# A two-block transformer step on one core: the ring of streamed weights, six slots of 1 MB or four

## What is computed

```python
# block 1: modulation from c; then, on h = norm(x) * (1 + scale) + shift
proj   = h @ w_in                       # 1024 x 7712, in column groups
y_att  = attention(q, k, v)             # 8 heads, keys of latent and context
y_gla  = gated_linear_attention(...)    # 4 heads, both directions
y_hy   = hyena_mix(u)                   # 2 long convolutions, as DFT products
x      = x + gate * (sum_b sigmoid(g_b) * (y_b @ w_br_b)) @ w_out
x      = x + gate * grouped_moe(h2)     # 16 experts, 3 matrices of 1024 x 512 each, top 2
# block 2
y_lru  = (gelu(h @ w_g) * rg_lru(conv(h @ w_x))) @ w_lru_out
y_dil, y_mem = dilated attention, attention over a memory of 256 tokens
x      = x + (gated sum of the three) @ w_out
x      = x + square(relu(hm @ w_mlp_in)) @ w_mlp_out     # 1024 x 4096 x 1024
return rms_norm(x)
```

## Time and profile before

| what | value |
|---|---|
| median of 3 runs | 2804.03 us (2803.7 to 2805.57) |
| the profiled execution: its own time | 2803.01 us |
| its span, first to last instruction | 2801.2 us |
| busy, share of the span | PE 88%, PEld 56%, DVE 40%, ACT 28%, POOL 12% |
| mean granted clock of PE, share of full | 0.92 |
| moved by DMA | 303.32 MB, mean 108 GB/s |
| DMA engines busy in the expert stage (slices 20 to 23 of 40) | 90% or more |

### The profile page before, as it was taken

The page is one execution under the profiler, slowest core; times in us unless marked ns, Lnnn a source line. Parts: engine busy times, 40 slices in busy tenths (PEclk is TensorE's granted clock), DMA queues, the critical chain, the costliest instruction groups (busy, mean ns, idle before and its releaser), DMA issues. The chain is left out here.

```text
span 2801.2 us, 22860 instructions
## 1 busy us (share of the span) xinstructions
PE 2464.0 (88%) x9040; PEld 1580.9 (56%) x9040; DVE 1110.4 (40%) x1481; ACT 772.2 (28%) x1070; POOL 327.4 (12%) x132
## 2 busy tenths in 40 slices
PE   5998989998989999885999738999869998499997
PEld 2446634543433666564887624445636666388885
DVE  2134376621423322225988641521562223522223
ACT  3131113212111211124877521520521112222121
POOL 0000000000000222211000000000012222344340
PEclk9996899999989899987999959999969999799999
DMA  5203113311111222205999921132102222232200
GB/s 202 96 31 153 39 60 123 118 53 35 38 34 53 83 90 90 90 31 213 378 394 394 369 69 51 60 109 60 46 21 70 94 87 75 66 114 87 93 31 30
DMA packets 177753, 303.32 MB, mean 108 GB/s; under 512 B 10205, under 2 KB 67592, under 8 KB 177652
## 3 DMA queue, kind: packets, MB, share of 16 engines
q1 hardware_dynamic: 171988, 283.07, 28.9%
q0 software_dynamic: 3360, 10.48, 1.1%
q10 hardware_dynamic: 2304, 8.39, 0.7%
HBM read 278.78 MB, written 23.13 MB: 108 GB/s over the span
## 5 line engine op out<-in xcount | busy, mean ns | idle before, releaser
L190 PE MATMUL ps<-region 128*128 128x512 f32 x1024 | 411.1, 401 | 79.2 <-DVE region L2771 35.5
L180 PE MATMUL ps<-region,weights 128*128 128x512 f32 (+3 forms) x1056 | 436.8, 573 | 34.3 <-PEq L376 17.9
L192 PE MATMUL ps<-region 128*128 128x512 f32 x1024 | 404.0, 395 | 0.0
L191 PE MATMUL ps<-region 128*128 128x512 f32 x1024 | 403.3, 394 | 0.0
L180 PEld LDWEIGHTS ps<-region,weights 128*128 128x128 f32 (+1 forms) x1056 | 198.4, 190 | 263.4 <-issue 255.9
L172 PE MATMUL ps<-region,weights 128*128 128x512 f32 x720 | 321.5, 602 | 3.0 <-DVE region L1421 3.0
L190 PEld LDWEIGHTS ps<-region 128*128 128x128 f32 x1024 | 195.7, 191 | 125.0 <-POOL region L1504 39.0
L1993 DVE TENSOR_TENSOR region<-weights,region 128x2048 fp32r<-128x2048 f32 x96 | 217.4, 2288 | 53.1 <-ACT region L1932 52.7
L172 PEld LDWEIGHTS ps<-region,weights 128*128 128x128 f32 x720 | 136.2, 192 | 169.2 <-issue 164.5
L192 PEld LDWEIGHTS ps<-region 128*128 128x128 f32 x1024 | 195.2, 191 | 42.1
L191 PEld LDWEIGHTS ps<-region 128*128 128x128 f32 x1024 | 196.1, 191 | 38.8
(11 more groups left out here) (348 smaller groups left out, 2645.5 us busy)
## 6 DMA issues: line engine op xcount, KB each, us to landing
weights<-w_in SPq DMA_DIRECT2D x54, 1024.0 KB, 5.2
weights<-moe_w_gate SPq DMA_DIRECT2D x32, 1024.0 KB, 13.0
weights<-moe_w_up SPq DMA_DIRECT2D x32, 1024.0 KB, 13.5
weights<-moe_w_down SPq DMA_DIRECT2D x32, 1024.0 KB, 12.9
weights<-w_mod SPq DMA_DIRECT2D x24, 1024.0 KB, 5.4
weights<-w_mlp_in SPq DMA_DIRECT2D x16, 1024.0 KB, 5.2
weights<-w_mlp_out SPq DMA_DIRECT2D x16, 1024.0 KB, 5.0
h_slots<-region SPq DMA_DIRECT2D x16, 512.0 KB
```

The costliest lines, as they stand in the source:

```text
L180: ins = pe.matmul(out, w[:, k % 4, col:col + m], x[:, k, tokens], start=(k == 0), stop=(k == KD - 1))
L190: pe.matmul(out, w_hi, x_hi, start=(n == 0), stop=False)
L191: pe.matmul(out, w_hi, x_lo, start=False, stop=False)
L192: last = pe.matmul(out, w_lo, x_hi, start=False, stop=(n == len(triples) - 1))
```

## The change

The ring gets four slots in place of six, and the wait of the MLP's loop on a slot's arrival counts the uses of a slot in one round of the loop from RING: 12 chunks in four slots are three uses (48) where they were two (32).

```diff
@@ -20,7 +20,7 @@
 CT = NCTX // P
 EPS = 1e-6
 HALF = 512
-RING = 6
+RING = 4
 NMARKS = 16
 NSIG = 24
 
@@ -2731,7 +2731,7 @@
         def _(act):
             def high(c, i):
                 n = n0 + c
-                act.wait_ge(r.arrived[n % RING], i * 32 + r.arrival(n))
+                act.wait_ge(r.arrived[n % RING], i * (16 * BC // RING) + r.arrival(n))
                 if c >= CH:
                     act.wait_ge(spent, i * BC + c - CH + 1)
                 act.activation(flat(part(c, 0)), raw(c)[:, :], ACT.Copy).then_inc(w_hi_done, 1)
```

## The result

| | before | after |
|---|---|---|
| median, range (4 runs each) | 2803.86 us (2801.22 to 2805.57) | 2834.97 us (2831.97 to 2838.28) |
| the profiled execution: time, span | 2803.01, 2801.2 us | 2833.9, 2832.1 us |
| busy PE, mean granted clock | 88%, 0.922 | 87%, 0.922 |

The ratio is 1.0112, with a 95% interval of 1.0095 to 1.0130: slower by 31 us. The forecast was 2831, with a range of 2817 to 2848. The page of after, as the earlier trace rows: the same instructions, and in the four slices of the expert stage 361 to 383 GB/s where 369 to 394 stood.

What follows compares the result with a forecast made beforehand. PE was taken to bound nearly everywhere, the weight stream perhaps in the expert stage. Opening 0.6, Hyena 14.1, recurrent 9.0 and expert 3.6 sum to 27.3 us on 2803.0, forecast as a 2831 us median; range 2817 to 2848.

Steps and rivals of the forecast that it cites:

- The rule k + 2: Whole ring: chunk k is issued when chunk k + 2 was before; hidden in projection, merge and MLP stages.
- The wait for Si: Hyena stages: Si is issued only after C, Sm and Ed are released; PE starts each inverse transform 4.8 us late.
- Its clock: Hyena stages: PE runs at its lower clock behind each gap before the inverse transform, 2.9 us each, bounds 0 and 5.
- Small loads: Start of the recurrent stage: small loads on SP land behind 2 MB of weights instead of 1 MB, +1.0 us.
- Second group: Recurrent stage: all four chunks of the second group are issued only when the first group is released, +3.0 us.
- qm: Recurrent stage: the two chunks qm are issued at the second release and land later than PE wants them, +3.0 us.
- The clock's +2.0 behind qm: Recurrent stage: two idle gaps close together before qm's matmuls lower PE's clock, +2.0 us, bounds 0 and 3.4.
- The 5.3 us of the two chunks: Expert stage: it starts with four chunks instead of six, so 92 instead of 90 are streamed in it, +5.3 us.
- Kept full, with 0.7 us to spare: Expert stage: a slot's round of 9.9 us against 10.6 us until its next chunk is due keeps the stream full.
- the stream runs thin: Expert stage rival: DVE and ACT hold slots too long, often one chunk under way; +15 us, 2846 us, chance 0.13.
- The gather: End of the expert stage: fewer chunks queued behind the last weight, so the gather waits less, -2.7 us.
- The opening stage: Opening stage: x comes after the fourth chunk, leaving PE more to do when the last lands, +0.6 us.

Runs made afterwards that it cites:

- w4_dft: Kernel before (six slots), but the chunks of the two Hyena stages issued only four ahead; 2814.91 us, ratio 1.0043.
- w4_lru: Kernel before (six slots), but the chunks of the recurrent stage, with the two of qm, issued only four ahead; 2808.64 us, ratio 1.0019.
- w5_moe: Kernel before (six slots), but the chunks of the expert stage issued only five ahead; 2807.31 us, ratio 1.0008.
- w4_moe: Kernel before (six slots), but the chunks of the expert stage issued only four ahead; 2818.84 us, ratio 1.0054.
- w3_moe: Kernel before (six slots), but the chunks of the expert stage issued only three ahead; 2854.37 us in its one run, beside 2802.38.
- rows_late4: Changed kernel, but in the expert stage DVE splits the next chunk before the rows of the next expert; 2830.71 us, ratio 1.0112.
- no_si: Changed kernel, but the Hyena inverse transform reads Ci in place of Si and awaits Si only at its end (wrong output); 2819.19 us, ratio 1.0065.
- halves4: Changed kernel, but ACT and DVE split each expert-stage chunk in two halves, DVE starting while ACT writes the second; 2824.05 us, ratio 1.0081.

## Why the prediction was right, point by point

**The rule k + 2, and where it costs nothing.** Held. In the profile of after PE waits for a weight in the Hyena and recurrent stages only where I said, and in no projection, merge or MLP stage.

**The wait for Si.** 4.8 us forecast, 5.0 and 4.8 measured, by the step of the prediction: release, 0.3 us, one landing. **Its clock** was mis-sized: 2.9 us each, carried over from one row, measured 1.4 and 2.5 in after, and 3.0 and 2.85 in w4_dft. One row of a clock's fall is a sample, not a price. **The loads before it**: -1.3 forecast, -2.0 measured, within the bounds.

**The recurrent stage.** Small loads +1.0, measured +1.7; PE's idle time there is 8.66 us in before, 10.51 in after and 10.30 in w4_lru, where only these chunks come late. Second group +3.0, measured +3.4 less 1.3 us of clock, where I held that the clock was "paid already": a longer gap was followed by a smaller loss at the lower clock. qm +3.0, measured 3.0 by the shift. The clock's +2.0 behind qm was wrong: 27.71 us for 64 matmuls is the 27.63 of before, although 1.45 and 2.81 us of idle time lie close together before them. Sum +9.0, measured +7.5, of which 0.7 is a slower start of the matmuls behind the small loads.

**The expert stage** is the step that failed. The 5.3 us of the two chunks hold (w5_moe: one chunk fewer, 2.4 us more). "Kept full, with 0.7 us to spare" and +1.0 for the rest do not: it was 15.3 less 5.3, about 10 us, in after, and 8.5 in w4_moe (from first to last split). I had named it a sign of being wrong if the stage moved clearly under 390 GB/s; it moved 379, so by my own sign this part was wrong, though the time came out in the range. Two things were wrong in that working. The round was built with the landing of a chunk that has the engines to itself, 5.6 us, and compared with a time that holds only if they are full; but in a full stream a chunk shares them, and lands after 7.6 to 8.9 us. And the pair, where the second lands 2.6 us behind the first, says at what rate a started queue drains; it doesn't say that two under way keep it at that rate, and w3_moe shows 343 GB/s for two on the mean. So the rival "the stream runs thin" was the right mechanism, at two thirds of its price. Its reason, that DVE makes other work before the worst chunk, does not carry the loss (rows_late4). The estimate of 60 us from the Trainium skill, "DMA: Bandwidth & Descriptors", section "Bandwidth", is six times what four slots lose; with three, where the stream comes nearest to one of single chunks, 43.5 us were lost.

**The gather.** -2.7 forecast, -2.5 measured, and w4_lru shows that it is the later issue of the chunks behind the experts' that gives it.

**The opening stage** had the wrong sign: +0.6 forecast, -1.9 measured. PE in after:

```profile
29.57 3.67 PE L225 MATMUL ps<-weights,silu_c 128*32 128x512 f32 x16
33.16 2.05 PE L232 MATMUL ps<-both,region 128*128 128x2 f32 x16
```

and in no_si, which is the same kernel up to here:

```profile
29.52 3.64 PE L225 MATMUL ps<-weights,silu_c 128*32 128x512 f32 x16
33.09 3.57 PE L232 MATMUL ps<-both,region 128*128 128x2 f32 x16
```

The last chunk was no longer waited for: x, which now comes after the fourth chunk, moved the 4 us pause from before the seventh chunk to before the fifth, and PE had the last two chunks without a break. The last 16 L232 take 2.05 us at its end, and 3.58 in before, and that is the clock. In no_si the last two chunks come without a break too, but the 16 L232 take 3.57 us, and PE is behind this stage 0.4 us sooner than in before and not 1.9. So the moved pause gives some 0.4 us; the other 1.5 are the clock's, which rose here in one execution and not in the other.

**The sum.** The misses cancel: against my terms the opening stage gave -2.5, the Hyena stages -3.6 and the recurrent one -1.5, the experts' +9.0, and small shifts in places that the change doesn't touch +2.0. So that 2831 lies so near to 2835 is luck in part: the experts' term was short by 9 us, and three others were too long by 7.6 together.

**What stays open.** Why the stream falls just once in each expert. It is the place where the rows of the next expert and the results of the last go between the weights, and the chunk before comes late; whether that traffic or the grouping of the six chunks makes it was not separated. The number of chunks ahead sets the loss (w5_moe, w4_moe, w3_moe); that the time for which a slot is held does too is likely (halves4) and wasn't told from the spread of the stage.

## What to carry to other kernels

To size a ring, don't build a slot's round with the landing of a lone chunk. The landing in a running stream grows with what stands in the queue (6.5 us with three chunks ahead, 8 with four, 14 with six), so it can't be carried from one number of slots to another either. Ask for the number under way that keeps the rate (here 4 MB under way, which took five slots, where the round with a lone chunk's landing gave four). Then count, stage by stage, how many chunks are held together: where that is more than the slots, or where all of a group are released at once, the next landing is bare, and releasing in pairs, or ordering the products so that one chunk is done with early, hides it at no cost that these runs show. Such a group costs time with the larger ring too: look for an idle gap of PE that ends by a weight's landing right behind a group's release.

## What the runs showed of the hardware

The rate of the DMA engines by MB under way, for chunks of 1 MB: 343 GB/s at 2.2 MB, 379 to 388 at 3.1, 394 at 4.2 and at 5.6. What a pause costs in PE's clock varies: idle gaps of 5.6 to 6.0 us were followed by 1.4 to 3.0 us of loss, 7.1 us by 1.6 (15.54 for 13.90), 3.73 us by 2.95, and 1.45 and 2.81 us together by none.
